# Two reorderings in a chunked recurrence: ScalarE's token copies ahead of a Gelu, VectorE's reciprocal ahead of other work

## The reference, cut to what matters

```python
def _gmlp_mixer(zu, zv, ln_w, ln_b, ws, bs):
    u = jax.nn.gelu(zu)
    v = layer_norm(jax.nn.gelu(zv)) * ln_w + ln_b
    mixed = einsum('hts,bcshd->bcthd', tril(ws), v in chunks of 128) + bs
    return u * mixed

def step(state, inp):                    # the recurrence, 8 heads of 64
    sa = einsum('bhvk,bhk->bhv', state, a_t)
    state = state * w_t + sa * b_t + v_t * k_t
    return state, einsum('bhvk,bhk->bhv', state, r_t)

y = group_norm(y) * gn_w + gn_b          # per head, (y - m) * rsqrt(var + eps)
y = (y + bonus) * g                      # g: the gate
```

## Time and profile before

| | |
|---|---|
| median of 3 runs | 2402.63 us (2402.24 to 2405.5) |
| the profiled execution | 2390.91 us, span of its core 2389.1 us |
| TensorE busy | 2248.4 us, 94% of the span |
| VectorE busy | 1223.7 us, 51% |
| ScalarE busy | 803.5 us, 34% |
| GpSimd busy | 374.6 us, 16% |
| HBM read | 383.13 MB |

### The profile page before, as it was taken

The page is one execution under the profiler, slowest core; times in us unless marked ns, Lnnn a source line. Parts: engine busy times, 40 slices in busy tenths (PEclk is TensorE's granted clock), DMA queues, the critical chain, the costliest instruction groups (busy, mean ns, idle before and its releaser), DMA issues.

```text
span 2389.1 us, 34462 instructions
## 1 busy us (share of the span) xinstructions
PE 2248.4 (94%) x14680; PEld 1632.4 (68%) x14680; DVE 1223.7 (51%) x1601; ACT 803.5 (34%) x1193; POOL 374.6 (16%) x247
## 2 busy tenths in 40 slices
PE   8998998997789979999899999999999999999998
PEld 5677875322223327877677699898787669989976
DVE  5785444300000007365865598486454739938745
ACT  3533222110011105123452354243342836424424
POOL 1001001100011000000000154262100024615310
PEclk9999989999999999999999999999999999999999
DMA  7224217999999994222121123333232012233330
GB/s 298 67 87 174 95 54 285 405 421 420 418 419 420 420 380 158 89 94 83 36 71 56 59 91 100 109 105 109 106 101 76 1 53 80 96 108 107 109 112 36
DMA packets 59021, 388.77 MB, mean 163 GB/s; under 512 B 7739, under 2 KB 7867, under 8 KB 17008
## 3 DMA queue, kind: packets, MB, share of 16 engines
q1 hardware_dynamic: 52896, 375.29, 41.2%
q0 software_dynamic: 5104, 8.09, 0.9%
q10 hardware_dynamic: 864, 3.15, 0.4%
HBM read 383.13 MB, written 13.63 MB: 166 GB/s over the span
## 4 chain that ended last, share of the span: by engine, by line
PE 79%; DMA 10%; DVE 6%; ACT 2%; SPq 1%; issue 1%; POOL 0%; DVEq 0%; POOLq 0%; ACTq 0%
PE psD L3550 39%; PE psD L2652 8%; PE psA L2652 8%; DMA ring<-w_moe 7%; PE psD L1415 7%; PE psA L3550 3%; DMA arena<-w_moe 1%; PE psA L1415 1%; SPq L795 1%; PE psA L2636 1%; DVE ring_r L3149 1%; PE psA L3625 1%; PE psD L3558 1%; PE psA L3782 1%; ACT ring_r L2928 1%
## 5 line engine op out<-in xcount | busy, mean ns | idle before, releaser
L3550 PE MATMUL psD<-rounded,ring_r 128*128 128x512 f32 (+1 forms) x3192 | 762.6, 399 | 6.4 <-DVE ring_r L3149 3.2
L3550 PEld LDWEIGHTS psD<-rounded,ring_r 128*128 128x128 f32 (+1 forms) x3192 | 596.3, 188 | 167.5 <-issue 16.6
L1415 PE MATMUL psD<-ring,arena 128*32 128x512 f32 x1568 | 178.9, 599 | 33.4 <-DMA ring<-w_moe 32.7
L3149 DVE TENSOR_TENSOR ring_r<-ring,ring_r 128x2048 fp32r<-128x2048 f32 (+2 forms) x71 | 159.0, 2239 | 83.4 <-ACT ring_r L2928 81.3
L2652 PE MATMUL psD<-rounded,fast_r 128*128 128x256 f32 x1680 | 199.5, 279 | 0.0
L2652 PE MATMUL psA<-rounded,fast_r 128*128 128x256 f32 x1680 | 199.3, 279 | 0.0
L2652 PEld LDWEIGHTS psA<-rounded,fast_r 128*128 128x128 f32 x1680 | 197.8, 188 | 0.4
L2652 PEld LDWEIGHTS psD<-rounded,fast_r 128*128 128x128 f32 x1680 | 197.6, 188 | 0.1
L2928 ACT ACTIVATE ring_r<-ring 128x2048 fp32r<-128x2048 f32 (+2 forms) x71 | 131.7, 1855 | 192.8 <-PE psD L3550 172.8
L1415 PE MATMUL psD<-arena 128*32 128x512 f32 x1504 | 171.7, 596 | 24.1 <-DMA arena<-w_moe 22.0
L3550 PE MATMUL psD<-rounded,fast_r 128*128 128x512 f32 x792 | 185.4, 395 | 0.0
(11 more groups left out here) (559 smaller groups left out, 2678.9 us busy)
## 6 DMA issues: line engine op xcount, KB each, us to landing
ring<-w_dense SPq DMA_DIRECT2D x134, 1024.0 KB, 5.1
ring<-w_moe SPq DMA_DIRECT2D x49, 2048.0 KB, 34.6
arena<-w_moe SPq DMA_DIRECT2D x47, 2048.0 KB, 33.9
ring<-w_dense SPq DMA_DIRECT2D x16, 768.0 KB, 4.3
ring<-w_dense SPq DMA_DIRECT2D x16, 640.0 KB, 3.9
arena<-pair_rows SPq DMA_DIRECT2D x8, 512.0 KB, 7.8
arena<-x_t SPq DMA_DIRECT2D x1, 2048.0 KB, 8.2
token_rows<-arena ACTq DMA_DIRECT2D x4, 512.0 KB, 10.9
```

Source lines behind the costliest of these rows:

```text
L1415: mm = pe.matmul(bank_[32 * g:32 * g + 32], rows(g), weights(g), start=start, stop=stop_)
L3149: dve.tensor_tensor(lo_, src, hi, ALU.subtract).then_inc(sem("w_lo"), 1)
L3550: mm = pe.matmul(out, w[a], x[b], start=start and i == 0, stop=stop_ and i == 2)
```

## The change

It has two parts, and no instruction is added or dropped.

On ScalarE the two Gelus of `zu` become a function, `spatial_gate`, which is called in chunk 0 behind `diagonals(0)` and ahead of `halfway_5(0)`. The token copies `by_tokens(0)` and the first modulation row's copy come ahead of `diagonals(0)`; before, they stood behind it.

On VectorE the reciprocal `scales(d - 1)` moves from behind `diagonals(d + 1)` and `columns(d, 1)` to directly behind `level_6(d)`, in chunks 1 to 3. In chunk 3 `yc_lo` moves from ahead of `level_6` to behind the reciprocal.

```diff
@@ -3012,10 +3012,12 @@
                    .then_inc(group_freed(("zv", h)), 1)
             ahead.leave(("zv", 1))
             root(small[:, 48:52])
-            group_ready(act, ("zu", 1))
-            for h in range(2):
-                act.activation(YC[:, 2 * h:2 * h + 2, :], dbank(("zu", h)), ACT.Gelu_apprx_tanh)\
-                   .then_inc(group_freed(("zu", h)), 1)
+            def spatial_gate():
+                group_ready(act, ("zu", 1))
+                for h in range(2):
+                    act.activation(YC[:, 2 * h:2 * h + 2, :], dbank(("zu", h)), ACT.Gelu_apprx_tanh)\
+                       .then_inc(group_freed(("zu", h)), 1)
+
             def diagonals(d):
                 act.wait_ge(sem("consts"), 3)
                 act.wait_ge(sem("lm"), 1)
@@ -3052,6 +3054,9 @@
                 act.activation(dst, src, ACT.Copy).then_inc(sem("chain_free"), 1)
 
             for d in range(NCH + 1):
+                if d == 0:
+                    by_tokens(d)
+                    mod_row(1, 0, 0, MROW)
                 if d < NCH:
                     diagonals(d)
                 if d > 0:
@@ -3067,8 +3072,7 @@
                 if d == NCH:
                     break
                 if d == 0:
-                    by_tokens(d)
-                    mod_row(1, 0, 0, MROW)
+                    spatial_gate()
                 halfway_5(d)
                 if d > 0:
                     by_tokens(d)
@@ -3485,16 +3489,17 @@
                 columns(d, 0)
                 if d > 0:
                     asked_at = variance(d - 1)
+                level_6(d)
+                if d > 0:
+                    scales(d - 1, asked_at)
                 if d == NCH - 1:
                     yc_lo(0, CONV_P[1], YC[:, 0:4, :], CONV_P[0])
-                level_6(d)
                 if d + 1 < NCH:
                     diagonals(d + 1)
                 else:
                     ahead(last_unit(("w_out", 0)))
                 columns(d, 1)
                 if d > 0:
-                    scales(d - 1, asked_at)
                     normed(d - 1)
             ahead.limit = N_FIRST - 1
             ahead(last_unit(("w_out", 1)))
```

## The result

| | before | after |
|---|---|---|
| median, first set of runs | 2401.03 us (2387.0 to 2405.5, 8 runs) | 2380.26 us (2378.28 to 2388.65, 8 runs) |
| ratio | | 0.9937 (95%: 0.9917 to 0.9957) |
| profiled execution | 2390.91 us | 2378.28 us |
| span of the profiled execution | 2389.1 us | 2376.6 us |

The change makes the kernel faster. By the medians of this set it is 20.8 us, by the ratio 15; a second set gave 2381.6 against 2393.08 us, 11.5 us, ratio 0.9956 (0.9939 to 0.9974). The first set's median of before holds the three runs of the forecast (2402.24 to 2405.5), which lie high: over all 99 other runs of before the median is 2393.6 us, and over all 20 of the changed kernel 2380.7. The gain is thus some 11 to 13 us. The forecast was 2391.6 us with a range of 2386.0 to 2396.8; the time lies under the range.

What follows compares the result with a forecast made beforehand. TensorE was taken as the bound, carrying 79% of the chain, so only its idle time could shrink. Gains of 3.0 + 1.5 + 2.5 + 4.0 = 11.0 us off the 2402.63 us median gave 2391.6 us, range 2386.0 to 2396.8.

Steps and rivals of the forecast that it cites:

- All four waits: TensorE idle 3.51 us ahead of chunk 0's masks, and 1.41, 1.66, 3.84 us ending chunks 1, 2, 3.
- the three put down to "issue": Waits before the head-spreading product in chunks 1 to 3; forecast tied them to the reciprocal, ending 0.16 to 0.17 us earlier.
- Part 1: ScalarE, ahead of chunk 0: earlier token copies start the mask product sooner; 3.0 us taken, ends 2.2 and 3.5.
- Part 2: VectorE, chunks 1 and 2: earlier reciprocal; 1.5 us (1.2 to 1.9) and 2.5 us (2.2 to 2.9) taken.
- Part 3: VectorE, chunk 3: rounding goes behind last level's copy and reciprocal; 4.0 us taken, ends 3.4 and 7.3.
- The remaining stall: Chunk 3, TensorE behind u0, ahead of the first output product: a wait for VectorE of about 3.2 us stays.
- The sum: Gains 3.0 + 1.5 + 2.5 + 4.0 = 11.0 us, ends 9.0 and 15.6, taken off the median 2402.63 us.
- The rule: Short bursts with waits between run at dropped clock; used against chunk 3's upper end and for a slower rival.
- B: Rival: new gaps cost more clock than the old; 5 to 7 us gain remains, about 2396.5 us; chance 0.13.
- C: Rival: moved copies and reciprocal don't start early; only 0 to 4 us gained, about 2401 us; chance 0.08.
- D: Rival: gap behind u0 keeps the clock low into the output products; slower, about 2409 us; chance 0.05.

Runs made afterwards that it cites:

- after: First profile of the changed kernel, both parts of the change against the kernel before: profiled execution 2378.28 us, median of its set 2380.26 us, ratio 0.9937.
- scalar_only: Changed kernel with VectorE's order of before, so only ScalarE's part of the change: 2396.02 us, ratio 1.0004 to the kernel before.
- split_filled: Changed kernel with the first output weights' split ahead of chunk 3's multiplies, plus idle matmuls in the remaining waits: 2373.61 us, ratio 0.9930.
- before_again: Kernel before, unedited, timed against itself: 2392.47 us, ratio 0.9989; its profiled execution was the slowest of 13, 2408.48 us.
- filled_after: Changed kernel with idle matmuls put in TensorE's remaining waits: 2379.23 us, ratio 0.9939.
- split_first: Changed kernel with VectorE's split of the first output weights moved ahead of chunk 3's column add and three multiplies: 2377.14 us, ratio 0.9928.

## Why the prediction was right or wrong

**What bounds, right.** All four waits were read to their true releaser; the three put down to "issue" were the reciprocal's, and all three went when it moved.

**Part 1, right in most profiles.** 3.0 us were taken. Chunk 0 shrank by 3.0 in five of the eight profiles with this part, and by 1.7 to 1.8 in the other three (after, scalar_only, split_filled), where the clock fell during the last mask product. The lower end of 2.2 was half a microsecond too high. The Gelus cost nothing.

**Part 2, starts right, sizes too large.** Chunk 1: 1.5 taken, 1.0 to 1.1 measured. Chunk 2: 2.5 taken, 1.1 measured, outside the bounds of 2.2 to 2.9. In after the multiplies start at 264.44 - 259.79 = 4.65 us behind the last level's product; in before that was 273.04 - 266.18 = 6.86; so the 2.2 us are there. What failed is that both ends of the term let the work behind the wait run at least as fast as before. The clock falls as far behind the last level's product as before (269.9 - 266.2 = 3.7 us, now 263.6 - 259.8 = 3.8) and is low for the same 6.8 us, but the work now comes sooner: the low stretch covers less idle time and more work, the spreading product's end, the mask product and the start of u0, and takes half of the gain back.

**Part 3, right in mechanism, slightly too large.** 4.0 us taken, 3.7 measured for the stage to y, of which 0.5 are lost in the rest (11.5 against 11.0): 3.2 net, just under the lower end of 3.4. The remaining stall was forecast at 3.2 us and is 2.99, and the clock fell in it.

**The sum, near by luck.** 11.0 us against 10.5 to 15 (ratios 0.9956 and 0.9937). The recurrence gives 7.1 to 8.2 us, under the lower end of 9.0: chunk 2 was put 1.4 us too high, chunk 1 some 0.5, part 3 0.8 and, in the first profile, part 1 1.3. That the whole came out near 11 is, in the second profile of the changed kernel, due to the 2.4 us behind the recurrence, which the sum did not hold and no run explains. The forecast also read the waits' cost from one execution in which the clock had come back ahead of the chain in chunks 1 and 2; before_again loses another 14 us in chunks 1 to 3 (161.6 - 144.8, less 2.7 in chunk 0), behind the same waits.

**The step that failed.** "Nothing in the sum depends on that distance, so I take it off the median." The 11.7 us between the profiled execution (2390.91) and the median of three runs (2402.63) were not a constant that belongs to this kernel. Before's other medians are 2393.08, 2394.99 and 2393.42 us, and of its 99 other runs only 9 lie at 2402 us or more, where all three of those runs lay. The median of the 99 is 2393.6 us: the base was 9 us too high, and from the right one the same sum gives 2382.6, against 2380.7 over all runs of the changed kernel. That the first three runs all lay there was bad luck; to take three runs for the kernel's median and their scatter (3 us, where the kernel's runs reach from 2387 to 2408) for its scatter was the error. Why they took so long is not known, as none was profiled. The one long execution that was (2408.48 us) lost 16.8 of its 17.6 us in the very stage that the change alters, so the distance was not independent of the sum either. The sum made against the profiled execution, 2390.91 - 11.0 = 2379.9 us, would have met the 2380.26, but with a recurrence term that was 3 to 4 us too large.

**The rule, weighed on one side only.** The Trainium skill's section on HAM oscillation (TensorE: Matmul & The Clock Gate) says, of a kernel that waits for transfers between short bursts, that each next burst starts cold. The traces agree in part: in chunk 2 of before the product behind the wait of 1.66 us ran at the lower clock, while behind the 1.41 us of chunk 1 the first product still took 1.12 us and the clock fell 1.1 to 1.2 us after its start. And the clock also fell with no wait at all (after at 263.6, filled_after at 265.5, split_first at 297.7 us), which that sentence does not cover. The prediction used the rule only against the new gap; it speaks as much for removing the old ones.

**The rivals.** B had its mechanism in one place: the drop takes back part of the starts, in chunk 2. Over the whole recurrence the time at the lower clock fell instead (25.7 to 18.3 and 21.9 us). C and D did not come: the clock was back at 0.95 in the window from 311 to 315 us.

## What to carry to other kernels

A short wait of TensorE between short products costs its own length plus what the clock does behind it, and the second part differs from one execution to the next: here the stages behind waits of 1.4 and 1.7 us took 5 and 7 us more in one profile than in two others. Not every fall of the clock has a wait ahead of it, so removing all waits need not hold it. Count a stage's idle time and its busy time at the lower clock apart; here the two explained the stage to within 1.6 us in ten profiles. When a profiled execution lies far from the median of a few runs, don't carry the distance over as a constant: take more runs first, and ask whether the stage that is changed makes it. Before trusting a removed stall, follow the engine that comes next (here VectorE's weight split) and reorder that too: in chunk 3 that took another 3.4 us off the stage, about as much as the change itself had (3.7).

## What the runs showed of the hardware

The same program with the same wait of 1.41 us has the clock back at 1.00 some 3 us after its fall in two profiles and stays at 0.50 for some 20 us in a third, while TensorE's records show it busy but for 0.22 us of that time, with products of 64, 128 and 256 columns. The clock also fell behind 8 to 12 us in which TensorE was busy without a break, with small products (after at 263.6 us, filled_after at 265.5, split_first at 297.7). Two idle matmuls in each of the waits of 1.41 and 1.66 us, 1.88 us together, held the clock at 1.00 in chunks 1 and 2, over remaining waits of 1.16 us; the longest time of 11 runs was 2393.1 us, against 2402.2 of the 17 of before in that set. What decides whether the clock falls, and between the short and the long stretch, was not settled: no run moved a wait in time alone, and none made the small products denser without filling a wait.
